# Two requests for the exp-and-log table, an earlier gate product and a longer lag of the second weight chunk in the hybrid layers' projections

## The reference, cut to what matters

```python
proj = jnp.einsum("btd,de->bte", x, w_in)
(dn_q, dn_k, dn_v, dn_z, dn_b, dn_a, g_q, g_k, g_v, g_z, g_r) = _split(proj, IN_SIZES)
dn_qkv = jax.nn.silu(causal_short_conv(jnp.concatenate([dn_q, dn_k, dn_v], axis=-1), conv_w))
q = l2norm(cq...) * (DN_DK ** -0.5)      # x * rsqrt(sum(x * x) + 1e-6)
k = l2norm(ck...)
...
gate_logits = jnp.einsum("btr,re->bte", g_r, gla_gate_w2) + gla_gate_b
log_f = (jax.nn.log_sigmoid(gate_logits) / GLA_TAU)
...
attn = jnp.einsum("bhnid,bhnjd,bhnijd->bhnij", qc, kc, dec)   # dec: exp of differences of cumsum(log_f)
```

## Time and profile before

| | us |
|---|---|
| median of three runs | 2411.68 |
| the profiled execution | 2410.51 |
| its span (first to last instruction) | 2408.4 |
| TensorE busy | 2106.0 (87%) |
| VectorE busy | 1164.2 (48%) |
| ScalarE busy | 914.7 (38%) |
| projections of the first hybrid layer | about 15 to 244 |

### The profile page before, as it was taken

One profiled execution on the slowest core, in us unless ns is written; L12 is line 12 of the kernel. 1 busy time (PEld: TensorE's weight loads), 2 busy tenths in 40 slices (PEclk: granted clock), 3 DMA queues, 4 the chain that ended last, 5 costly groups with the idle time before them and its releaser, 6 DMA issues. The chain is left out here.

```text
span 2408.4 us, 28383 instructions
## 1 busy us (share of the span) xinstructions
PE 2106.0 (87%) x11432; PEld 1626.7 (68%) x11432; DVE 1164.2 (48%) x1427; ACT 914.7 (38%) x1257; POOL 346.2 (14%) x332
## 2 busy tenths in 40 slices
PE   7996788799769959988889999979997868999996
PEld 4775586477548638734667788757886746778875
DVE  4444645444464551244367547533113756754753
ACT  4237333624732342255344224323222624432431
POOL 1200623020063300033210000020000022000002
PEclk9998799899979979999999999999999979999998
DMA  5111002221100212100112232212222001223221
GB/s 198 70 70 53 2 18 89 80 79 70 53 1 2 105 37 103 70 1 1 70 70 88 73 112 92 86 59 93 99 88 70 1 35 70 86 74 112 88 90 59
DMA packets 27158, 163.53 MB, mean 68 GB/s; under 512 B 2755, under 2 KB 6267, under 8 KB 11420
## 3 DMA queue, kind: packets, MB, share of 16 engines
q1 hardware_dynamic: 27036, 161.81, 18.9%
HBM read 155.47 MB, written 6.33 MB: 67 GB/s over the span
## 5 line engine op out<-in xcount | busy, mean ns | idle before, releaser
L251 PE MATMUL psum<-inputs_high,weights_high 128*128 128x512 f32 x928 | 376.5, 406 | 5.1 <-DVE inputs_low L232 5.1
L253 PE MATMUL psum<-inputs_high,weights_low 128*128 128x512 f32 x928 | 363.8, 392 | 0.0
L252 PE MATMUL psum<-inputs_low,weights_high 128*128 128x512 f32 x928 | 363.8, 392 | 0.0
L237 DVE TENSOR_TENSOR weights_low<-weights_raw,weights_high 128x2048 fp32r<-128x2048 f32 x72 | 169.4, 2353 | 324.7 <-ACT weights_high L226 324.7
L1771 PE MATMUL psum<-inputs_high,weights_high 128*128 128x512 f32 x704 | 278.8, 396 | 19.9 <-DVE weights_low L1763 11.1
L1772 PE MATMUL psum<-inputs_low,weights_high 128*128 128x512 f32 x704 | 275.7, 392 | 0.0
L1773 PE MATMUL psum<-inputs_high,weights_low 128*128 128x512 f32 x704 | 275.5, 391 | 0.0
L251 PEld LDWEIGHTS psum<-inputs_high,weights_high 128*128 128x128 f32 x928 | 175.6, 189 | 57.4 <-DVE inputs_low L232 7.9
L252 PEld LDWEIGHTS psum<-inputs_low,weights_high 128*128 128x128 f32 x928 | 175.6, 189 | 38.5 <-issue 3.8
L253 PEld LDWEIGHTS psum<-inputs_high,weights_low 128*128 128x128 f32 x928 | 175.5, 189 | 37.5
L1756 ACT CAST weights_high<-weights_raw 128x2048 fp32r<-128x2048 f32 (+1 forms) x76 | 126.7, 1669 | 178.1 <-PE psum L1773 174.8
(11 more groups left out here) (317 smaller groups left out, 3360.8 us busy)
## 6 DMA issues: line engine op xcount, KB each, us to landing
weights_raw<-w_stream SPq DMA_DIRECT2D x116, 1024.0 KB, 4.8
weights_raw<-w_down SPq DMA_DIRECT2D x32, 704.0 KB, 4.1
residual_parked<-residual SPq DMA_DIRECT2D x2, 2048.0 KB, 11.1
residual_back<-residual_parked SPq DMA_DIRECT2D x2, 2048.0 KB, 7.9
residual<-x_t SPq DMA_DIRECT2D x1, 2048.0 KB, 7.9
out_t<-residual SPq DMA_DIRECT2D x8, 256.0 KB, 2.0
constants<-consts SPq DMA_DIRECT2D x1, 1537.5 KB, 11.7
table_backward<-bias_rows SPq DMA_DIRECT2D x1, 1024.0 KB, 5.5
```

What stands on the lines that cost most here:

```text
L237: dve.tensor_tensor(self.wlo[:, u, 0:self.cols], self.raw[:, u, 0:self.cols], self.whi[:, u, 0:self.cols].bitcast(F32), ALU.subtract).then ...
L251: pe.matmul(out, hi, self.ahi[:, k], start=start and b == 0, stop=False)
L252: pe.matmul(out, hi, self.alo[:, k], start=False, stop=False)
L253: mm = pe.matmul(out, lo, self.ahi[:, k], start=False, stop=stop and b == blocks - 1)
```

## The change

Four edits in `hybrid_projections`: `behind` goes from 2 to 3; the gate product moves from step 4 to step 0; `exp_and_log` is called ahead of ScalarE's wait for the small product, and again in chunk 12 ahead of `inverse(0)`.

```diff
-                behind = 2
+                behind = 3
                 for step in range(KD + behind):
...
-                    if step == 4:
+                    if step == 0:
                         pe.wait_ge(s.small_out, 1)
                         for f in range(2):
                             mm = pe.matmul(ps[:, 6 + f], h.w2[0:16, f * P:(f + 1) * P], small[0:GATE_RANK, :],
...
                 st.input_high(act, s, 2, 5)
+                exp_and_log(act)
                 act.wait_ge(s.small, 1)
                 act.copy(small[:], ps[0:N_SMALL, 4]).then_inc(s.small_out, 1)
...
                     elif c == 12:
+                        exp_and_log(act)
                         for j in range(4):
                             inverse(j)
```

## The result

The changed kernel takes 2367.73 us (median of four runs, 2366.26 to 2368.64) against 2411.59 us; the ratio is 0.9821 with a 95% interval of 0.9804 to 0.9838. The forecast was 2367.6, with 2358 to 2377 as range.

The account below looks back on a forecast made before the run. TensorE, busy 87%, was taken as the bound except at its waits and at phase ends, where ScalarE works on alone. Late 17.7 plus early 4.3 us a layer, 44.1 us in two layers, gave 2367.6 us, range 2358 to 2377.

Parts of the forecast that it names:

- The bound and the late part: End of each projection phase: 16 loads become one, the limit passes from ScalarE to TensorE, 17.7 us a layer earlier.
- the queue's own distance from a matmul to a sum: Late sums on TensorE: the queue itself puts about 0.33 us, so sums 5, 6 and 7 each give back 0.93.
- The requests hold: Chunk 12: after the request, Ln and Exp run with no load between; the rival that it fails, 2408 us, chance 0.025.
- The gate product: Step 0: runs behind 6 matmuls instead of 48, 9.6 us earlier; TensorE does not wait, VectorE's decays done by 39.
- The lag of three: Chunk 2's low part: ready at 48.1, 0.9 us ahead of TensorE; a lag of two would leave a 0.5 us wait.
- What is late next: `pair(2)` waits 1.3 us for `take(0)`, behind the low part of chunk 3; the early gain is 4.3 us a layer.
- That the clock would stay full: At `pair(2)`: the 1.3 us wait does not lower TensorE's clock; otherwise four us at half clock cost 2.0.
- The sum: Both layers: 17.7 + 4.3 = 22.0 us a layer, 44.1 us in all; profiled execution 2366.4, median 2367.6 us.
- a later phase longer than before by more than 2 us: In the profile after: one of the signs that would show the prediction wrong.
- rival (c): End of each phase: shorter idle time brings TensorE into the next at full clock, 2 us or more a layer; chance 0.07.

Follow-up runs that it names:

- experiment 1: The kernel before with only the second request, in chunk 12 (gate product in step 4, lag of two, no first request): 2377.93 us, ratio 0.9843.
- experiment 7: The changed kernel with the second request moved between the two taps of chunk 12: 2367.70 us, ratio 0.9825.
- experiment 2: The changed kernel without the second request, in chunk 12: 2404.14 us, ratio 0.9951.
- experiment 3: The changed kernel with both requests, but the gate product in step 4 and a lag of two as before the change: 2371.20 us, ratio 0.9817.
- Experiment 5: The changed kernel with a lag of two instead of three: 2367.20 us, ratio 0.9816.
- Experiment 4: The changed kernel without the first request, ahead of the wait for the small product: 2375.06 us, ratio 0.9823.
- experiment 6: The changed kernel with `take(0)` ahead of the low part of chunk 3 in VectorE's order: 2367.74 us, ratio 0.9810.
- experiment 10: The changed kernel with `take(0)` ahead of the low part of chunk 3 and without the first request: 2365.12 us, ratio 0.9801.
- the repetition: The changed kernel run again, unaltered: 2366.98 us, ratio 0.9813; its profiled execution took 2362.93 us.

## Why the prediction was right

**The bound and the late part.** Right: 16 loads became one and the limit passed to TensorE (experiments 1 and 7). 17.7 us were reckoned and 18.2 measured. The term that was off is the queue's own distance from a matmul to a sum: I took 0.33 us from a small group of another shape; the trace after has 0.23 (206.99 to 207.22), and from sum to sum 3.02, 2.93 and 2.93 us instead of the 3.1 that I reckoned, 0.45 of the 0.5 us.

**The requests hold.** No load stands between Ln and Exp in the middle of the stream. Experiments 1 and 2 measured 18.2 us a layer on the second request. By the rule of the Trainium skill (ScalarE activation tables: per-element evaluation and per-set limits, Table sets in the compiler and the runtime) that the compiler places the loads by the greedy longest run, there would have been nothing to gain late; the trace does not agree. The load occupies 1.28 us and the next instruction starts 0.01 later (202.08 to 203.37). The drain of about 1380 ns that the Trainium skill (ScalarE: Activation LUTs, What ACT_TABLE_LOAD costs) adds to each load is not in this trace.

**The gate product.** Moved as reckoned: it starts 1.6 us behind the first projection matmul (25.27) instead of 11.1, and TensorE did not wait in front of it. Its effect, VectorE through with the decays early, was right as well. But experiment 3 shows how little it and the lag together bring once the requests are there: 0.6 us a layer.

**The lag of three.** The prediction set it against a wait of 0.5 us. Experiment 5 measured the wait (0.39), and that it costs nothing, since the wait at `pair(2)` gives it back. The prediction left out this comparison, though its own numbers held it: with chunk 2 starting at 49.5, `pair(2)` is reached 8.1 us later, at 57.6, still before `take(0)` ends at 58.3.

**What is late next.** Right in place and size: `take(0)` behind the low part of chunk 3, 1.15 us for 1.3, no fall of the clock, 4.34 us gained for 4.3. That the size fits to 0.1 us is in part luck, since the half clock of the execution before is counted in it, and in experiment 1 that was 1 us shorter. Experiment 4 makes this wait longer, experiments 6 and 10 take it away: from `pair(3)` on, the marks of the phase move with it to 0.1 us (2.9 us later in experiment 4, of which 1.5 is the clock; 1.1 to 1.2 earlier in 6 and 10). That the clock would stay full was taken from one wait of 1.68 us. It came true here, but it is no rule: the wait of 1.99 us shown below was followed by a full clock once and by half clock 23 times.

**The sum.** 22.6 us a layer for 22.0, 45.2 us for 44.1. The medians fell by 43.9 us and the profiled executions by 42.1. So the forecast's agreement to 0.1 us comes out of two errors against each other: the phases gained more than reckoned, and the rest of the program, put at nothing, was longer in the profiled execution. The prediction named "a later phase longer than before by more than 2 us" as a sign of being wrong, and the 2.6 us between the phases are such a sign; in the repetition it is 0.7 us. The 2.6 us can be followed from instruction to instruction. The table gives four stretches between the phases (us):

| | before | after | after, repeated |
|---|---|---|---|
| last silu to the first product with the delta rule's state (L1053 before, L1055 after) | 79.0 | 78.9 | 78.5 |
| from there to the sums of the layer norm, behind the output projection (L1320 before, L1322 after) | 94.5 | 95.9 | 95.8 |
| from there to layer 2's small product (L428) | 24.6 | 27.0 | 24.6 |
| from there to the first projection matmul | 9.7 | 8.6 | 9.7 |

The first stretch answers rival (c): behind the shorter idle time at the end of the phase it took as long as before. In the second, TensorE waits for 1.99 us in front of L1053, in every profile and in both layers. The stretches around its start, first in the kernel before, layer 1 and layer 2, and then in the kernel after, layer 1 (us, busy us of PE, PEld, DVE, ACT, POOL, then the granted clock):

```profile
322.17 1.16 PE L1053 MATMUL psum<-state,k_beta_g 128*128 128x128 f32 x8 [1.99 <-DVE gla_state L1080]
...
321.00:327.00 6.00, 4.83 (x41) 4.76 (x42) 1.66 (x3) 0.58 (x1) 0.00 (x0) 1.00 0.01 3
...
746.00:752.00 6.00, 4.29 (x26) 4.29 (x27) 1.83 (x4) 0.00 (x0) 0.00 (x0) 0.72 0.01 3
```

```profile
297.70:303.70 6.00, 5.00 (x30) 5.00 (x31) 1.58 (x3) 0.44 (x1) 0.00 (x0) 0.72 0.01 3
```

The kernel before kept full clock here in layer 1 and not in layer 2, where it took 95.8 us too. In all twelve profiles, two layers each, it is the only pass with a full clock. So 1.4 of the 2.6 us come from one lucky pass in the profile of before, and not from anything the changed kernel does worse. The third stretch, the layer norm, cost 2.4 us in the one profiled execution of the changed kernel and nothing in the repetition. A stretch of 30 us with nearly the same work (the last blocks of the output projection and this layer norm), in the kernel before, after, and in the repetition of the latter:

```profile
407.00:437.00 30.00, 17.02 (x51) 9.57 (x49) 11.19 (x18) 12.64 (x19) 2.55 (x2) 0.88 0.00 0
```

```profile
385.00:415.00 30.00, 19.21 (x50) 10.15 (x49) 11.17 (x18) 11.05 (x17) 2.56 (x2) 0.77 0.00 0
```

```profile
384.00:414.00 30.00, 16.39 (x48) 9.10 (x46) 11.18 (x18) 12.64 (x19) 2.56 (x2) 0.87 0.00 0
```

The granted clock was 0.88, 0.77 and 0.87. So neither loss needs the change: each place shows both times in one and the same kernel. Over the profiled executions of all these kernels the stretch between the phases took 207.9 to 211.7 us, and the one behind them up to TensorE's last matmul 1720.0 to 1726.2; the 1.4 us lost in the latter were not followed. As the kernel before has one profile, and the lowest time of all between the phases, it is not shown that the rest of the program is untouched on average; what is shown is that its executions differ by more than that.

## What to carry to other kernels

Count the table loads of ScalarE in the groups' view. Where two functions alternate and each brings a load, one request for a set that holds both shortens ScalarE's chain until another engine bounds it, and no further. Behind a removed wait, follow every engine's written order to the next instruction that is late: here it was a small copy that stood behind the making of a whole chunk's low part, and it made the lag edit worthless and one hidden-looking load cost 2.9 us a layer. And where edits are worth 1 us in 2400, read marks inside the phase; the medians move by more for other reasons.

## What the runs showed of the hardware

A wait of TensorE of 1.80 us (experiment 3) was followed by a full clock, one of 2.56 us (experiment 4) by 1.2 GHz, which cost 1.5 us on top. The length of the wait alone does not decide it: the same wait of 1.99 us at L1053 was followed by a granted clock of 1.00 in the first layer of the kernel before and of 0.50 to 0.72 in the 23 other passes, and the stretch behind it took 94.5 us against 95.8 to 97.5. The same wait of 3.1 us at chunk 2 cost 1.0 us more behind it in the profiled execution of before than in experiment 1. Two profiled executions of the changed kernel differed by 5.5 us with every mark of the changed phases equal to 0.15 us, and in the 30 us around the first layer norm the granted clock differed by 0.10.

A table load took 1283 ns each time and nothing beside it: behind a load the next instruction started 0.01 to 0.02 us later, and load, Ln, load and Exp took 4.03 us where Ln and Exp behind the request took 1.34 (experiment 1 and the kernel after against the kernel before).
